# Attention values with the values as left operand, in a hybrid HGRN2 and sliding-window attention layer on one Trainium2 core

## The reference, cut to what matters

```python
def sink_attention(q, k, v, mask, sink):
    s = jnp.einsum('bnqhgd,bnchd->bnhgqc', q, k).astype(jnp.float32) * (HEAD_DIM ** -0.5)
    s = jnp.where(mask[None, :, None, None], s, NEG_BIG)
    ...
    prob = jax.nn.softmax(jnp.concatenate([s, sink_col], axis=-1), axis=-1)[..., :-1]
    return jnp.einsum('bnhgqc,bnchd->bnqhgd', prob.astype(v.dtype), v)

def merge(att_o, ga, hg_o, gh, hg_norm_w, w_out):
    att = att_o.reshape(*lead, ATT_WIDTH) * jax.nn.silu(ga)
    hg = rms_norm(hg_o, hg_norm_w).reshape(*lead, HG_WIDTH).astype(gh.dtype) * jax.nn.silu(gh)
    return jnp.concatenate([att, hg], axis=-1) @ w_out
```

## Time and profile before

| | us |
|---|---|
| median of 3 runs | 1169.42 |
| lowest and highest | 1166.57, 1173.78 |
| the profiled execution | 1172.12 |
| its span (first to last instruction) | 1170.3 |
| granted TensorE clock, mean over the span | 0.985 of 2.4 GHz |

### The profile page before, as it was taken

One profiled execution on the slowest core, in us unless ns is written; L12 is line 12 of the kernel. 1 busy time (PEld: TensorE's weight loads), 2 busy tenths in 40 slices (PEclk: granted clock), 3 DMA queues, 4 the chain that ended last, 5 costly groups with the idle time before them and its releaser, 6 DMA issues.

```text
span 1170.3 us, 26019 instructions
## 1 busy us (share of the span) xinstructions
PE 1134.5 (97%) x9490; PEld 946.9 (81%) x9490; DVE 717.3 (61%) x1845; ACT 430.7 (37%) x1242; POOL 366.9 (31%) x425
## 2 busy tenths in 40 slices
PE   6999999999999999999899999999999999889998
PEld 4787888888888888887668888888888888678887
DVE  6657666666666666668745565555656666745443
ACT  6402222222222222216124555455556665423230
POOL 0003333333333333334412232222322237523331
PEclk9989999999999999999998999999999999989999
DMA  8531111111111111127113312111111134343431
GB/s 281 180 109 58 63 65 63 63 63 63 63 62 55 63 63 63 46 82 272 48 66 134 140 45 79 55 45 45 62 69 51 46 120 158 117 146 144 147 140 72
DMA packets 49391, 108.33 MB, mean 93 GB/s; under 512 B 5088, under 2 KB 17888, under 8 KB 49312
## 3 DMA queue, kind: packets, MB, share of 16 engines
q1 hardware_dynamic: 49328, 107.51, 25.8%
HBM read 70.23 MB, written 38.26 MB: 93 GB/s over the span
## 4 chain that ended last, share of the span: by engine, by line
PE 88%; DVE 7%; issue 2%; POOL 1%; ACT 1%; DMA 1%; DVEq 0%; SPq 0%; ACTq 0%; POOLq 0%
PE h_bank_b L919 5%; PE h_bank_a L919 5%; PE h_bank_b L921 5%; PE h_bank_b L920 5%; PE h_bank_a L921 5%; PE h_bank_a L920 5%; PE o_bank L2634 4%; PE o_bank L2636 4%; PE o_bank L2635 4%; PE h_bank_t L903 3%; PE a_bank_b L1894 3%; PE a_bank_a L1894 3%; PE a_bank_a L1895 3%; PE a_bank_a L1896 3%; PE a_bank_b L1895 3%; PE a_bank_b L1896 3%
## 5 line engine op out<-in xcount | busy, mean ns | idle before, releaser
L919 PE MATMUL h_bank_b<-h_w_hi,h_h_hi 128*128 128x512 f32 x256 | 106.4, 416 | 0.1
L1684 DVE CUSTOM_DVE_ANT_0 a_sm<-a_sc,a_hidden,a_neg_sink 128x272 f32<-128x272 f32 x128 | 59.0, 499 | 75.4 <-PE a_sc L1924 75.3
L919 PE MATMUL h_bank_a<-h_w_hi,h_h_hi 128*128 128x512 f32 x256 | 103.1, 403 | 0.0
L921 PE MATMUL h_bank_b<-h_w_hi,h_h_lo 128*128 128x512 f32 x256 | 100.7, 393 | 0.0
L920 PE MATMUL h_bank_b<-h_w_lo,h_h_hi 128*128 128x512 f32 x256 | 100.2, 391 | 0.0
L921 PE MATMUL h_bank_a<-h_w_hi,h_h_lo 128*128 128x512 f32 x256 | 99.9, 390 | 0.0
L920 PE MATMUL h_bank_a<-h_w_lo,h_h_hi 128*128 128x512 f32 x256 | 99.9, 390 | 0.0
L1490 ACT ACTIVATE a_prb<-a_sm,a_neg_m 128x256 f32<-128x256 f32 x128 | 64.2, 502 | 70.5 <-DVE a_neg_m L1684 70.4
L1894 PE MATMUL a_bank_a<-a_w_hi,a_h_hi 128*128 128x512 f32 (+1 forms) x208 | 77.0, 370 | 0.3 <-DMA a_h_lo<-h_split 0.3
L1894 PE MATMUL a_bank_b<-a_w_hi,a_h_hi 128*128 128x512 f32 (+1 forms) x200 | 75.2, 376 | 0.0
L1895 PE MATMUL a_bank_a<-a_w_lo,a_h_hi 128*128 128x512 f32 (+1 forms) x208 | 74.1, 356 | 0.0
(11 more groups left out here) (328 smaller groups left out, 3164.1 us busy)
## 6 DMA issues: line engine op xcount, KB each, us to landing
h_split<-h_h_hi SPq DMA_DIRECT2D x17, 512.0 KB, 3.0
h_split<-h_h_lo SPq DMA_DIRECT2D x17, 512.0 KB, 3.8
a_h_hi<-h_split SPq DMA_DIRECT2D x17, 512.0 KB, 3.5
a_h_lo<-h_split SPq DMA_DIRECT2D x17, 512.0 KB, 4.3
h_x<-x_prompt SPq DMA_DIRECT2D x16, 512.0 KB, 3.3
o_m<-mixed SPq DMA_DIRECT2D x16, 512.0 KB, 4.1
o_x<-x_prompt SPq DMA_DIRECT2D x16, 512.0 KB, 4.1
y_prompt<-o_x SPq DMA_DIRECT2D x16, 512.0 KB, 2.6
```

The source lines that it names most:

```text
L919: pe.matmul(out[:, :], h_hi[t.slot][:, k, :], hi, start=(k == 0), stop=False)
L921: ins = pe.matmul(out[:, :], h_lo[t.slot][:, k, :], hi, start=False, stop=(k == KT - 1))
L1684: ins = dve.tensor_tensor_reduce(SM[j % 2][:, i, :], sc[:, i, 0:KEYS], hidden[:, mask, :], -SCALE, neg_sink[:, h:h + 1], ALU.add, ALU.min, ...
```

## The change

`values` runs twice a tile instead of four times, and its operands change sides: the left operand is 64 columns of `V`, the moving one 256 columns of turned probabilities, two heads of one key group. The heads of a step are now one of each key group, j and 4 + j. The output comes out turned, with the 64 dimensions of the two key groups in the two halves of the partitions. It is copied to `MIX` by ScalarE (`copy_o`, new), turned back by TensorE (`turn_o`, new, four transposes), divided by VectorE from `bank_o` into `MIX`, and multiplied by the gate there; `o_nat` is gone. The meta product becomes four products with 128 columns. `turn_p` of a step moves behind the scores of the next. The orders of all engines are written anew around this, in the loop, in the first tile and at the end. In the output stage, the low parts of sum 0 move from GpSimd to VectorE; VectorE splits sums 2 and 0 ahead of `sum_1`, and the samples' additions stand ahead of operand 5; the zeroing of the samples' buffer waits for the last but one tile's `o_ready` instead of `mix_done`, and `P1` lies behind that buffer.

```diff
-        PTS = sb("pts", [P, 2, 2 * P])
+        PTS = sb("pts", [P, KVH, 2, 2, P])
-        o_nat = sb("o_nat", [P, HW])
+        def head(j, kv):
+            return kv * G_HEADS + j
...
@@ attention: sync @@
-                store_mixed(tile(0, n))
+                if n < TILES - 3:
+                    store_mixed(tile(0, n))
             sp.wait_ge(kv_proj, TILES)
+            yield
+            store_mixed(tile(0, TILES - 3))
...
@@ attention: gpsimd @@
-                wait(pool, mix_stored, 16 * t.n)
-                pool.tensor_tensor(MIX[:, :], o_nat[:, :], G[t.slot][:, :], ALU.mult).then_inc(mix_done, 1)
+                pool.tensor_tensor(MIX[:, :], MIX[:, :], G[t.slot][:, :], ALU.mult).then_inc(mix_done, 1)
...
             def iteration(t0, t1, t2, last, tail=True, ahead=True, more=True):
+                if ahead:
+                    k_rstd_of(t1)
                 if tail:
                     mix(last)
                 if ahead:
-                    k_rstd_of(t1)
                     q_rstd_of(t1)
...
@@ attention: scalar @@
-                wait(act, pv_done, 4 * (t.n - 1) + j)
+                wait(act, pv_done, 2 * (t.n - 1) + j // 2)
...
-                act.activation(PTS[:, :, :], pt[:, :, 0:2 * P], ACT.Copy).then_inc(p_placed, 1)
+                act.activation(PTS[:, :, :, j % 2, :], pt[:, :, 0:2 * P].rearrange("p a (b q) -> p a b q", b=2),
+                               ACT.Copy).then_inc(p_placed, 1)
+
+            def copy_o(t):
+                act.wait_ge(o_ready, 2 * t.n - 1)
+                wait(act, mix_stored, 16 * t.n)
+                act.activation(MIX[:, :], bank_o[:, :], ACT.Copy).then_inc(o_copied, 1)
...
-                if tail:
-                    place_p(last, 3)
+                gate(t0)
                 place_q(t0, 0)
-                gate(t0)
+                place_p(last, 3)
                 place_q(t0, 1)
-                if ahead:
-                    keys_values(t1)
                 exps(t0, 0)
+                keys_values(t1)
+                copy_o(last)
                 place_p(t0, 0)
...
                 place_p(t0, 2)
+                place_k(t1)
                 exps(t0, 3)
-                place_k(t1)
                 sink_exp(t0)
...
             place_p(t0, 3)
             place_q(end, 0)
             gate(end)
+            copy_o(t0)
             place_q(end, 1)
...
             place_p(end, 3)
+            yield
+            copy_o(end)
...
@@ attention: vector @@
             def o_norm(t):
-                dve.wait_ge(o_ready, t.n)
+                dve.wait_ge(o_ready, 2 * t.n)
...
-                dve.tensor_tensor(heads(o_nat[:, :]), heads(bank_o[:, :]), rden[:, :].unsqueeze(2).to_broadcast([P, AH, HD]),
+                by_head = rden[:, :].rearrange("p (x g) -> p x g", x=KVH).unsqueeze(3).to_broadcast([P, KVH, G_HEADS, HD])
+                dve.tensor_tensor(MIX[:, :].rearrange("p (x g d) -> p x g d", x=KVH, d=HD),
+                                  bank_o[:, :].rearrange("p (g x d) -> p x g d", x=KVH, d=HD), by_head,
...
                 gate_plus(t0)
+                maxima(t0, 0, mask)
+                place_v(t0)
+                if ahead:
+                    k_stats(t1)
+                maxima(t0, 1, mask)
+                if ahead:
+                    k_norm(t1)
                 if tail:
                     o_norm(last)
-                place_v(t0)
-                maxima(t0, 0, mask)
-                if ahead:
-                    k_stats(t1)
-                    k_norm(t1)
-                maxima(t0, 1, mask)
                 gate_recip(t0, 0)
...
@@ attention: tensor @@
-            def values(t, j):
-                pe.wait_ge(p_placed, 4 * (t.n - 1) + j + 1)
+            def values(t, a):
+                pe.wait_ge(p_placed, 4 * (t.n - 1) + 2 * a + 2)
...
+                for block in range(2):
+                    for kv in range(KVH):
+                        c = slice(kv * HD, (kv + 1) * HD)
+                        ins = pe.matmul(bank_o[c, 2 * a * P:2 * (a + 1) * P], V[block][:, c],
+                                        PTS[:, kv, block, :, :].rearrange("p g q -> p (g q)"),
+                                        start=(a == 0 and block == 0), stop=False, skip_group_check=True)
...
-                if j == 3:
-                    pe.matmul(bank_o[:, :], PMT[:, :], VMD[:, :], start=False, stop=True).then_inc(o_ready, 1)
+                if a == 1:
+                    for g in range(G_HEADS):
+                        c = slice(g * P, (g + 1) * P)
+                        ins = pe.matmul(bank_o[:, c], VMD[:, c], PMT[:, :], start=False, stop=True, skip_group_check=True)
+                    ins.then_inc(o_ready, 1)
+
+            def turn_o(t):
+                pe.wait_ge(o_copied, t.n)
+                for g in range(G_HEADS):
+                    c = slice(g * P, (g + 1) * P)
+                    ins = pe.transpose(bank_o[:, c], MIX[:, c], ident[:, :])
+                ins.then_inc(o_ready, 1)
...
@@ attention: tensor, tile 1 @@
+            scores(t1, 1)
             turn_p(t1, 0)
-            scores(t1, 1)
...
             project(t2, kv_bank(t2), 2, range(0, 4))
-            pe.wait_ge(v_meta_spread, AH * 16)
+            scores(t1, 2)
+            turn_p(t1, 1)
             values(t1, 0)
...
+            project(t2, kv_bank(t2), 2, range(4, 8)).then_inc(g_proj, 1)
+            scores(t1, 3)
             turn_p(t1, 2)
-            scores(t1, 3)
             pe.wait_ge(q_placed, 2)
             turn_k(t2)
...
@@ attention: tensor, iteration @@
+                project(t1, kv_bank(t1), 0, range(0, 4))
+                pe.wait_ge(k_placed, t0.n + 1)
+                turn_q(t0, 0)
+                turn_p(last, 3)
...
+                scores(t0, 0)
+                values(last, 1)
...
+                project(t1, q_bank(t1), 1, range(0, 4))
+                scores(t0, 1)
                 turn_p(t0, 0)
+                turn_o(last)
+                project(t1, q_bank(t1), 1, range(4, 8)).then_inc(q_proj, 1)
+                scores(t0, 2)
                 turn_p(t0, 1)
...
                 project(t1, kv_bank(t1), 2, range(0, 4))
+                values(t0, 0)
+                scores(t0, 3)
                 turn_p(t0, 2)
...
                 project(t1, kv_bank(t1), 2, range(4, 8)).then_inc(g_proj, 1)
...
@@ output: gpsimd @@
-            yield
-            pool.wait_ge(attention["mix_done"], TILES)
+            pool.wait_ge(attention["o_ready"], 2 * (TILES - 1) - 1)
             pool.memset(s_rows[:, :, :].bitcast(F32), 0.0).then_inc(sums_made, 1)
...
+            yield
             sums(tile(0, 1))
-
-            for k in range(HK):
-                pool.wait_ge(w_high, W_DONE + 2 * KT + 2 * HK + k + 1)
-                pool.tensor_tensor(t_lo[0][:, k, :], t_raw[0][:, k, :], t_hi[0][:, k, :].bitcast(F32), ALU.subtract).then_inc(w_ready, 1)
...
@@ output: scalar @@
                 operand(0, bank_t[0][:, :])
+                if not p:
+                    split_sums(0, 1)
...
             rows_high(tile(0, 1), None)
-            split_sums(0, 1)
             split_sums(3, 4)
...
@@ output: vector @@
             operand(n, 0, bank_t[0][:, :])
+            split_sums(2, 1)
+            split_sums(0, 2)
             sum_1(n)
...
             sum_4(n)
-            split_sums(2, 1)
             add_x(tile(0, 1), 1)
             operand(n, 3, S3[:, :])
             operand(n, 4, S1[:, :])
+            for a in range(2):
+                add_sample(a)
             operand(n, 5, C22[:, :])
...
                     split_sums(3, 3)
-                    for a in range(2):
-                        add_sample(a)
...
@@ output: tensor @@
-            multiply(t1, 1, 0, 4)
+            multiply(t1, 1, 0, 2)
+            yield
+            multiply(t1, 1, 2, 4)
             turn_block(n, 0, None)
```

More of the change, by code:

```diff
@@ L1579, in scalar @@
             t0, end = tile(0, TILES - 2), tile(0, TILES - 1)
+            gate(t0)
+            place_q(t0, 0)
             place_p(tile(0, TILES - 3), 3)
-            place_q(t0, 0)
-            gate(t0)
             place_q(t0, 1)
+            exps(t0, 0)
             keys_values(end)
-            exps(t0, 0)
+            copy_o(tile(0, TILES - 3))
             place_p(t0, 0)
@@ L1844, in vector @@
             gate_plus(t0)
-            o_norm(last)
-            place_v(t0)
-            maxima(t0, 0, t0.slot)
-            k_stats(end)
-            k_norm(end)
-            maxima(t0, 1, t0.slot)
+            maxima(t0, 0, t0.slot)
+            place_v(t0)
+            k_stats(end)
+            maxima(t0, 1, t0.slot)
+            k_norm(end)
+            o_norm(last)
             gate_recip(t0, 0)
@@ L1865, in vector @@
             gate_plus(end)
+            maxima(end, 0, end.slot)
+            place_v(end)
             o_norm(t0)
-            place_v(end)
-            maxima(end, 0, end.slot)
             yield
@@ L2040, in tensor @@
-            values(t1, 2)
-            turn_p(t1, 3)
-            pe.wait_ge(k_placed, 3)
```

(35 more changed lines are left out.)

104 lines of the change are left out of this document (42 added, 62 removed).

## The result

The median of six runs after is 1150.20 us (1148.88 to 1151.52), of six runs of before 1169.59: a ratio of 0.983 with a 95% interval of 0.981 to 0.985, 19.4 us less.

What follows compares the result with a forecast made beforehand. TensorE's own work was taken to bound the loop, with other engines stopping it at the first tile and hand-over. Profiled 1172.1 - 4 (loop) - 0 (first tile) - 4.3 (hand-over) = 1163.8 us, median about 1161; range 1151 to 1174.

Steps and rivals of the forecast that it cites:

- What bounds the kernel: Whole kernel: in the attention loop only TensorE's own work counts; others stop it at the first tile and the hand-over.
- The step of values: Attention loop: a step's eight records need five slots, 1.12 us, and with the shape switch about 1.40 us.
- Rival 4: Values in the loop: four slots a step instead of five, another -6 us, 1155 us; chance 0.09.
- The other terms of a tile: Attention loop: meta product 0.90 us, turn_o 0.44; a tile's sum 4.14 against 4.40, about -4 us over 14 tiles.
- What should cost nothing: Attention loop: copy_o and the reordered work of other engines hide behind TensorE; later turns absorb the late step's 0.16 us.
- Tile 1: First tile of the loop: the 1.63 us wait goes, waits of 0.8 and 1.6 to 1.8 come; 0 us in sum.
- The hand-over: Attention to output stage: VectorE's addition 2.5 us earlier, TensorE's wait 3.4 us, half clock 1.0; together -4.3 us.
- rival 1: Values in the loop: the two halves run one after the other, a step 2.12 us, 1181 us; chance 0.10.
- rival 3: Hand-over: TensorE no longer waits before the fourth block and keeps its clock, 10.7 us instead of 4.3, 1155; chance 0.19.

Runs made afterwards that it cites:

- half by half: The changed kernel with the four products of a values step ordered by key group, both key blocks of one group first: 1150.85 us, ratio 0.9839 to before.
- turns first: The changed kernel with each turn_p of steps 0 to 2 ahead of the next step's scores again: 1149.34 us, ratio 0.9836 to before.
- sum 0 on GpSimd: The changed kernel with the low parts of sum 0 back on GpSimd, behind its first two sums: 1152.38 us, ratio 0.9858 to before.
- splits behind: The changed kernel with VectorE's eight splits of sums 2 and 0 behind sum_4 again: 1154.66 us, ratio 0.9871 to before.
- the run on one half: The changed kernel with both key groups written to the lower half of the output partitions: 1174.43 us, ratio 1.0042 to before.

## Why the prediction was wrong, step by step

- **What bounds the kernel**: right. TensorE is at 22.76 of 22.76 us in a tile at clock 1.00, so its own work is what shrinks, and the hand-over is where other engines stop it.
- **The step of values is the term that failed.** I wrote that both records of a product use the same half, "so the first and the last have no partner: eight records need five such slots". The count is four: the second product starts beside the first, whole product beside whole product. Measured are 1.01 from the first record to the next instruction and, from the groups of the two loops, 0.20 more in the projection's products around two steps of a tile (14.14 to 14.34 us), so 1.11 a step instead of 1.41. Four slots at the pace of one half's records, 0.216 us, are 0.86 of it instead of 1.12; the other 0.25 is the change of shape, for which 0.29 was kept, so that price was nearly right. Rival 4's price, 1.40 - 0.22 = 1.18, was the nearer one. Behind it stood a rule of the Trainium skill ("TensorE: Matmul & The Clock Gate", section "Measured speedup vs the span model"), and the trace agrees: the partner starts about 0.007 us later, where the page has about 4 ns for each further tile.
- **The trace of before could have decided it.** L954 was read as the nearest case, and its rows do not decide. But by its neighbour in the earlier trace rows, L945 with four groups, 32 records take 0.46 us. Could a record run beside the one in front of it and no other, as I assumed, they would need 17 slots of 0.46 / 16 = 0.029 us (the price by the meta row), which puts the last start at 0.46 already and the end its own 0.2 us later. And at L949, two groups like L954's, the very first record has a partner (two begun by 328.44, shown above).
- **The other terms of a tile**: the meta product 0.91 (0.90 foreseen), `turn_o` 0.36 (710.44 to 710.80; 0.44 foreseen). The tile's sum is 2 x 1.11 + 0.91 + 0.36 = 3.49 against 4.43 by the same groups before, so 0.9 less instead of 0.3 (22.76 against 23.65 for the whole tile). The stretch holds the values of 15 tiles, not 14: 15 x 0.89 = 13.4 us. Of the rest of the 14.1, the spell at half clock behind the old wait is gone (3.40 us at 0.50, 1.7 us), and the waits around the loop are 1.1 us longer, not shorter: 0.69, 2.06 and 0.66 instead of 1.63 and three of 0.2 to 0.3.
- **What should cost nothing**: right. There is no idle row on TensorE in the loop; `copy_o` ends 1.9 us ahead of `turn_o` (at 708.58, against 710.44). But the 0.16 us of the old late step was put down to the turn's place behind the scores, and the experiment says that this place brings nothing here; the loop's other reorderings did it, and which one was not tried.
- **Tile 1**: the two new waits are there, 0.69 and 2.06 (0.8 and 1.6 to 1.8 foreseen), so this term was no gain in waits. The half clock that can come behind such a wait does not come in the profile of the change; it does in four of the eight traces with this order of tile 1 (half by half, turns first, sum 0 on GpSimd and splits behind: 0.72 over the six us behind the wait of 2.06).
- **The hand-over**: the mechanism was right and each size a little off on the same side. GpSimd's differences end 28.4 us after the first output product instead of 24.0 (983.17 + 1.28 - 956.01 against the earlier trace rows; 4 foreseen), `sum_1` comes 2.8 us later (3.8 foreseen), since eight splits take 4.89 us and not 5.9, and from there to the addition it is 1009.40 - 994.04 = 15.4 us (15.9 foreseen). The wait is 1.67 instead of 3.4, and the half clock, for which I had kept 1.0, does not come: 7.0 us instead of 4.3. That GpSimd's splits slow VectorE, and that the idle stretch takes the splits, two experiments bear out.
- **The rivals**: rival 1 had the sign right and the price too high where it applies: with one half used, a step takes 1.87 us (2.12 foreseen), a tile 24.46, 0.81 more than before (1.18 foreseen), and the kernel is 0.4% slower than before. Rival 4 and half of rival 3 came true together. I had priced each of them alone, at 1155, and let the range end at 1151; nothing excluded both at once, and together they give 1161 - 6 - 3 = 1152. The last 2 us are not accounted for more closely: by the stretches of the two traces the gain is 21.1 us, by the medians 19.4.

## What to carry to other kernels

Where an operand is only 64 columns wide, put it on the left and give two independent sums the two halves of the output partitions: products of the two halves run beside each other in whole, and the order in which they are issued did not matter here. Price it by the pairs, and the switch between shapes by the neighbours' starts on either side. At a hand-over between stages, look first for the idle stretch of the engine whose chain ends last: putting the eight splits there is worth 5.8 us here, the whole new order 8.7 without any change in the attention ahead of it, and the addition that TensorE waits for belongs ahead of work that is needed later.

## What the runs showed that I had not expected

Each half of the output partitions seems to have its own order. With the products issued half by half, a record of the second half still starts beside the first of the first half, 0.013 us after it, two products ahead of its turn (0.007 us when it stands next). The records do not name their half; that the partner is of the other one follows from the run on one half, where no two records pair.

The clock can fall or stay at the same place without an edit there: among the samples' products it falls in every trace but that of turns first. Windows over the samples' products and what follows in tile 1, the change and then turns first:

```profile
606.90:618.55 11.65, 11.65 (x45) 7.24 (x45) 3.05 (x13) 1.95 (x9) 0.70 (x1) 0.71 0.07 23
```

```profile
605.70:617.40 11.70, 11.70 (x63) 8.06 (x63) 5.28 (x19) 3.82 (x16) 0.69 (x1) 1.00 0.16 48
```

Both are busy throughout; at 0.71 the one gets through 45 records, at 1.00 the other through 63. So turns first is 3.0 us ahead when the wait of 2.06 us ends (628.70 - 605.70 = 23.00 us behind the first mark, against 632.94 - 606.90 = 26.04). Behind that wait its own clock falls, and 1.5 us are left at the first meta product:

```profile
628.70 0.63 PE L1934 MATMUL a_bank_t<-c_ident,a_qs 128*128 128x128 f32 x4 [2.06 <-POOL a_qs L1400]
```

```profile
629.40:632.80 3.40, 3.40 (x19) 3.40 (x18) 0.72 (x3) 1.96 (x5) 0.00 (x0) 0.50 0.33 51
```

Half by half reaches it 1.5 us later than the change: it has the same spell here and a second one behind the wait of 2.06 us, with no idle time in it:

```profile
634.00:640.00 6.00, 6.00 (x36) 5.11 (x36) 1.07 (x5) 2.90 (x13) 0.00 (x0) 0.79 0.89 304
```

So a difference of 1.5 us between two traces is read by its place, not by its total.
